# Two more combined pairs in the feed-forward's first part of a hybrid encoder step, and two weight sums of every combined pair made by adding transfers

## The chip, the cores and the metric

The kernel runs on 1 core of a Trainium2 chip. The metric is the device time of one execution in microseconds. Engine names: PE is TensorE, DVE is VectorE, ACT is ScalarE, POOL is GpSimd, SP is SyncE, which here only issues transfers.

## The reference, cut to what matters

Two layers. Each projects 640 rows (512 prompt rows, 8 x 16 sample rows) of 1024 features, runs two attention branches, mixes them with gates and closes with the feed-forward part that is at issue here:

```python
def finish_layer(x, a, b, ga, gb, w_a, w_b, w_o, g1, b1, w_up, w_down, g2, b2):
    mix = (ga * (a @ w_a) + gb * (b @ w_b)) @ w_o
    x = layer_norm(ALPHA * x + mix, g1, b1)
    h = jnp.square(jax.nn.relu(x @ w_up)) @ w_down      # 1024 -> 4096 -> 1024
    return layer_norm(ALPHA * x + h, g2, b2)
```

All arrays are float32, D_MODEL is 1024, D_FF 4096, DEPTH 2.

## The kernel before, in words

**Products in halves.** Every float32 operand is split into a high part (rounded by a copy to fp32r, ACT) and a low part (the rest, a subtraction, DVE). A product is three matmuls that add up in PSUM: high x high, low x high, high x low. Weights come as chunks of 128 x 1024 (512 KB), two chunks (a pair n) at a time, into four raw slots (`load`, L489); SP loads a slot again when the low part of the chunk in it has been made (`w_ready`).

**Plain tiles.** `feature_tile` (L549 to L551) multiplies one chunk (128 output features) with all 640 rows, as two halves of 320 rows, 8 blocks of 128 inputs each.

**Combined pairs.** `combined_pair` on PE (L575 to L577) takes two chunks together as a 2 x 2 block matrix (two output tiles, two halves of the inputs, two halves of the rows) and makes it with seven block products in place of eight, by sums of blocks: four x sums t1 to t4 (made once and kept, `x_sums`, `x_sum_low`, `t_high`) and four weight sums per pair. The seven products, in order, go to five PSUM banks X1 to X5: X1 (part 0), X4 (part 1, the sum s_one, with t1), X2 (part 2, t2), X1 (part 3), X2 (part 4, t3), X3 (part 5), X5 (part 6, t4). ACT copies a bank into another between them (`up_seed`, L1600: seed 0 is X1 to X2 after the first product, seed 1 X2 to X3 after the third, seed 2 X2 to X5 after the fifth), and the later product adds onto the copy. The third product waits for seed 0, the fifth for seed 1, the seventh for seed 2. DVE makes the sums (`weight_sums`: L2400 s_one = a21 + a22, L2403, L2407, L2411), ACT the high parts (`part_highs`, L1573), DVE the low parts (`part_low`, L2420). s_one has one buffer. Each pair's weights are made during the pair before; the first pair's of a group before the group starts.

**The order.** Each engine's program is written out by hand and runs in order, with counted semaphores between them. Per layer: first head and v tiles, 4 combined pairs of gates, 8 heads of attention, 4 combined pairs of the branch product (BRANCH), window attention, second branch, mix and layer norm, then the feed-forward in 4 parts. A part makes 8 tiles of up features (4 pairs), squares of their relu, and multiplies them with 8 chunks of w_down (`row_group`, L642 to L644). In part 0 the four pairs are plain; in parts 1 to 3 they are combined. In part 0 ACT does relu (L1842) and the high part of the square (L1845), DVE the square (L2658) and its low part (L2661), and in between the x sums of that layer (L2359 to L2375, high parts L1539, low parts L2385) for part 1. Part 0's first pair is run by `first_tiles`, between the last transposes of the layer norm (L933), from weights kept aside; the second starts right behind it. GpSimd has no program of its own.

The lines of ACT's program for part 0:

```python
for u in range(FF_PAIRS):
    for s in range(2):
        act.wait_ge(chunk_done[s], nth(l, AT_FF) + u + 1)
        fn(halves(tmp1[:]), pair(s), ACT.Relu).then_inc(relu_done[s], 1)
        high(s, nth(l, AT_FF, 1) + u)
        fn(act_a[0][:, 2 * u + s, :], tmp2[:], ACT.Copy).then_inc(h_hi_ready, 1)
    for t in ((), (1,), (2, 3), (4,))[u]:
        t_high(l, 1, t)
```

## Time and profile before

| | us |
|---|---|
| median of 3 runs | 2186.23 (2185.57 to 2189.0) |
| the profiled execution | 2187.18 |
| its span | 2185.4 |
| PE busy | 2175.2 |
| DVE busy | 1408.0 |
| ACT busy | 1135.6 |
| POOL busy | 0.2 |

The span is the time from the first to the last record of the profiled execution. Busy is the time in which an engine had an instruction in work. Matmuls are pipelined, so a record (309 ns for 320 columns) overlaps the next; the distance from one start to the next is what one costs. A wait is put down to the engine that released it.

### The profile page before, as it was taken

Reading aid. Unit: us, or ns where it says so; the run is one execution under the profiler, and the core shown is the slowest. Engines: PE = TensorE matmul, PEld = TensorE weight load, DVE = VectorE, ACT = ScalarE, POOL = GpSimd, SP = SyncE. Lnnn points to the kernel's source line nnn. Section 1 sums busy time; section 2 is a strip of 40 time slices with the busy share of each in tenths; the row PEclk is TensorE's granted clock in tenths of the full one; section 3 lists DMA queues with packets and bytes.
Section 4 is the critical chain, followed back from the end, with each engine's and each line's share of the span. In section 5 each row is a group of like instructions: output and inputs, shape, how many; then the busy total and the mean of one; then the engine's idle time right before and its main releaser. Section 6 shows DMA issues by size and latency. Waiting matters only on the chain.

```text
span 2185.4 us, 38374 instructions
## 1 busy us (share of the span) xinstructions
PE 2175.2 (100%) x15290; PEld 1981.7 (91%) x15290; DVE 1408.0 (64%) x2324; ACT 1135.6 (52%) x2401; POOL 0.2 (0%) x4
## 2 busy tenths in 40 slices
PE   9999999999999999999999999999999999999998
PEld 8988889999989898989889888899999898989897
DVE  6757777776466573736667577786764665736466
ACT  4457776686323262626234677666853232626261
POOL 0000000000000000000000000000000000000000
PEclk9999999999999999999999999999999999999999
DMA  5366552431431222222233765525214312222231
GB/s 186 102 243 253 200 214 101 151 111 50 147 119 39 87 78 83 86 74 88 106 108 103 275 233 191 206 86 172 74 51 148 116 54 79 85 73 88 68 111 73
DMA packets 68160, 268.18 MB, mean 123 GB/s; under 512 B 10984, under 2 KB 12648, under 8 KB 61296
## 3 DMA queue, kind: packets, MB, share of 16 engines
q1 hardware_dynamic: 43136, 152.75, 20.5%
q10 hardware_dynamic: 24848, 112.99, 14.5%
q8 instruction: 122, 2.00, 0.4%
q14 instruction: 54, 0.44, 0.1%
HBM read 236.35 MB, written 25.95 MB: 120 GB/s over the span
## 4 chain that ended last, share of the span: by engine, by line
PE 99%; DVE 0%; DMA 0%; DVEq 0%; issue 0%; ACT 0%; ACTq 0%
PE PS L549 11%; PE PS L551 11%; PE PS L550 11%; PE PS L642 10%; PE PS L644 10%; PE PS L643 10%; PE PS L575 8%; PE PS L577 8%; PE PS L576 8%; PE PS L768 2%; PE PS L793 2%; PE PS L732 1%; PE PS L683 1%; PE PS L898 1%; PE PS L782 1%; PE PS L714 1%
## 5 line engine op out<-in xcount | busy, mean ns | idle before, releaser
L549 PE MATMUL PS<-xt_hi,w_hi 128*128 128x320 f32 x1312 | 420.7, 321 | 0.0
L551 PE MATMUL PS<-xt_hi,w_lo 128*128 128x320 f32 x1312 | 405.3, 309 | 0.0
L550 PE MATMUL PS<-xt_lo,w_hi 128*128 128x320 f32 x1312 | 405.1, 309 | 0.0
L1128 ACT ACTIVATE w_hi<-w_raw 128x1024 fp32r<-128x1024 f32 x194 | 203.6, 1058 | 361.8 <-PE PS L644 286.0
L1914 DVE TENSOR_TENSOR w_lo<-w_raw,w_hi 128x1024 fp32r<-128x1024 f32 x194 | 235.4, 1222 | 235.9 <-ACT w_hi L1128 232.3
L642 PE MATMUL PS<-w_hi,act_a_hi 128*128 128x512 f32 x800 | 312.2, 390 | 0.0
L644 PE MATMUL PS<-w_hi,act_a_lo 128*128 128x512 f32 x800 | 311.4, 389 | 0.0
L643 PE MATMUL PS<-w_lo,act_a_hi 128*128 128x512 f32 x800 | 311.4, 389 | 0.0
L549 PEld LDWEIGHTS PS<-xt_hi,w_hi 128*128 128x128 f32 x1312 | 246.6, 188 | 10.6 <-issue 8.0
L550 PEld LDWEIGHTS PS<-xt_lo,w_hi 128*128 128x128 f32 x1312 | 246.9, 188 | 0.1
L551 PEld LDWEIGHTS PS<-xt_hi,w_lo 128*128 128x128 f32 x1312 | 246.3, 188 | 0.0
L644 PEld LDWEIGHTS PS<-w_hi,act_a_lo 128*128 128x128 f32 x800 | 150.2, 188 | 31.5
L642 PEld LDWEIGHTS PS<-w_hi,act_a_hi 128*128 128x128 f32 x800 | 150.2, 188 | 30.9 <-issue 0.5
L643 PEld LDWEIGHTS PS<-w_lo,act_a_hi 128*128 128x128 f32 x800 | 150.2, 188 | 30.5
L1155 ACT ACTIVATE rope_s<-PS 32x320 f32<-32x320 f32 x352 | 150.6, 428 | 49.5 <-DVE z_all L1905 22.8
L2420 DVE TENSOR_TENSOR part_lo<-w_raw,part_hi 128x512 fp32r<-128x512 f32 x130 | 88.7, 689 | 57.1 <-ACT part_hi L1573 54.2
L1573 ACT ACTIVATE w_hi<-w_raw 128x512 fp32r<-128x512 f32 x110 | 66.3, 624 | 59.3 <-PE PS L644 48.5
L1573 ACT ACTIVATE part_hi<-w_raw 128x512 fp32r<-128x512 f32 x130 | 80.1, 623 | 27.9 <-DVE w_raw L2407 26.8
L2257 DVE SCALAR_TENSOR_TENSOR rows<-rows,PS 128x512 f32<-128x512 f32 x100 | 67.2, 685 | 34.0 <-PE PS L644 34.0
L575 PE MATMUL PS<-t_hi,part_hi 128*128 128x320 f32 x288 | 89.0, 309 | 0.0
L576 PE MATMUL PS<-t_lo,part_hi 128*128 128x320 f32 x288 | 89.0, 309 | 0.0
L577 PE MATMUL PS<-t_hi,part_lo 128*128 128x320 f32 x288 | 89.0, 309 | 0.0
(282 smaller groups left out, 4574.0 us busy)
## 6 DMA issues: line engine op xcount, KB each, us to landing
w_raw<-in_weights SPq DMA_DIRECT2D x274, 512.0 KB, 3.5
kc<-in_k_cache ACTq DMA_DIRECT2D x32, 1024.0 KB, 7.7
vc<-in_v_cache ACTq DMA_DIRECT2D x16, 2048.0 KB, 8.8
gates_kept<-a_t ACTq DMA_DIRECT2D x8, 640.0 KB, 7.0
k_out<-k_t ACTq DMA_DIRECT2D x16, 320.0 KB, 2.4
v_out<-rows ACTq DMA_DIRECT2D x2, 2560.0 KB, 16.9
mix_a<-a_t ACTq DMA_DIRECT2D x2, 2560.0 KB, 11.7
rope_c<-gates_kept ACTq DMA_DIRECT2D x10, 320.0 KB, 3.2
```

Of the source, the lines that this page charges most:

```text
L549: mm(out, wh, hi[:, k, c], start=(k == 0), stop=False)
L550: mm(out, wh, lo[:, k, c], start=False, stop=False)
L551: last = mm(out, wl, hi[:, k, c], start=False, stop=(k == KT - 1))
L575: mm(up_bank(x), wh, moving[0][:, k], start=first and k == 0, stop=False, skip_group_check=True)
L576: mm(up_bank(x), wh, moving[1][:, k], start=False, stop=False, skip_group_check=True)
L577: last = mm(up_bank(x), wl, moving[0][:, k], start=False, stop=(k == KH - 1), skip_group_check=True)
L642: mm(out, xh, wh, start=(k == 0), stop=False)
L643: mm(out, xh, wl, start=False, stop=False)
L644: last = mm(out, xl, wh, start=False, stop=(k == KT - 1))
L1128: fn(w_hi[slot][:], raw[:, j, :], ACT.Copy).then_inc(w_hi_made[s], 1)
L1155: last = fn(rope_s[dst:dst + 32, half * HALF:(half + 1) * HALF], PS[src:src + 32, bank_of(0, half), 0:HALF], ACT.Copy, scale=scale)
L1914: v.tensor_tensor(w_lo[slot][:], raw[:, raw_of(s, n)[0], :], w_hi[slot][:].bitcast(F32), ALU.subtract)\
```

## The change

Part 0 of the feed-forward runs its pairs 0 and 1 plain and its pairs 2 and 3 combined, in both layers, so that there are 44 combined pairs in place of 40. PSUM bank three (X2) holds other results until then, so one extra matmul with the start flag opens it ahead of the first combined pair of part 0. The x sums are made within the first two pairs. ACT now makes both squares of a plain tile's relu (the high part and the full square), and DVE only the low part.

Of the four weight sums of every combined pair, s_one and s_three (the sum in place of a21) are no longer made by DVE but by transfers of GpSimd's queue, which add in flight: `weights[2n, :, 0:512]` is added onto the raw slot of the second chunk, and s_one is loaded with a21, and after that has landed a22 is added. As a transfer can only add, the signs of two sums, of t3 and of two seeds are turned, and the takes (`up_add`) subtract where they added. Three semaphores of the attention heads become one. Cut to its core:

```diff
-BRANCH = FF_PARTS
-PAIR_ORDER = (0, BRANCH, 1, 2, 3)
-PAIR_GROUPS = len(PAIR_ORDER)
+PLAIN_PAIRS = 2
+GATES, BRANCH = FF_PARTS, FF_PARTS + 1
+
+
+def first_pair(part):
+    return 0 if part else PLAIN_PAIRS
+
+
+PAIR_ORDER = [(part, u) for part in (GATES, BRANCH, 0, 1, 2, 3) for u in range(first_pair(part), FF_PAIRS)]
+LAYER_PAIRS = len(PAIR_ORDER)
...
+        @block.gpsimd
+        def _(pool):
+            def pair_sums(l, part, u):
+
+                q, n = pair_at(l, part, u)
+                j, loads = raw_of(1, n)
+                pool.wait_ge(raw_loaded[j], 16 * loads)
+                pool.dma_start(raw[:, j, 0:BANK], weights[2 * n, :, 0:BANK], accum_op=ALU.add)\
+                    .then_inc(s_three_added, 16)
+                if q:
+                    pool.wait_ge(s_summed, 2 * q - 1)
+                    pool.wait_ge(part_ready, 5 * q - 3)
+                if (part, u) == (GATES, 0):
+                    if l == 0:
+                        pool.wait_ge(masks_ready, 2)
+                        pool.wait_ge(lam_link, 6)
+                    else:
+                        pool.wait_ge(input_rows, l * ROW_STEPS)
+                elif (part, u) == (BRANCH, 0):
+                    pool.wait_ge(unit_pv, 3 * HEADS * (l + 1))
+                    pool.wait_ge(dec_ms_ready, HEADS * (l + 1))
+                elif (part, u) == (0, PLAIN_PAIRS):
+                    pool.wait_ge(ln_rows, ROW_STEPS * (l + 1))
+                pool.dma_start(s_one[:], weights[2 * n + 1, :, 0:BANK]).then_inc(s_one_loaded, 16)
+                pool.wait_ge(s_one_loaded, 32 * q + 16)
+                pool.dma_start(s_one[:], weights[2 * n + 1, :, BANK:D], accum_op=ALU.add).then_inc(s_one_loaded, 16)
+
+            for l in range(DEPTH):
+                for part, u in PAIR_ORDER:
+                    pair_sums(l, part, u)
...
+                if renew is not None:
+                    pe.wait_ge(x_lo_ready, renew)
+                    mm(up_bank(X2), part_hi[0][:, 0:P], b11[0][:, 0], start=True, stop=True)
...
-                        if part > 0:
-                            if (part, u) == (1, 0):
-                                pe.wait_ge(t_lo_ready, sums_before(l + 1, 0))
-                                for s in range(2):
-                                    pe.wait_ge(relu_done[s], (l + 1) * FF_PAIRS)
+                    if part == 0:
+                        for u in range(1, PLAIN_PAIRS):
+                            for s in range(2):
+                                pe.wait_ge(relu_done[s], l * PLAIN_PAIRS + u)
+                                feature_tile(s, nth(l, AT_FF) + u, xt_hi, xt_lo, s)
+                    for u in range(first_pair(part), FF_PAIRS):
+                        if part == 0 and u == PLAIN_PAIRS:
+                            first_waits = {0: lambda: pe.wait_ge(relu_done[0], (l + 1) * PLAIN_PAIRS),
+                                           1: lambda: pe.wait_ge(relu_done[1], (l + 1) * PLAIN_PAIRS),
+                                           KH: lambda: None}
+                            combined_pair(*pair_at(l, part, u), sums_before(l, 2), first_waits=first_waits,
+                                          renew=tiles_before(l, 1) + ROW_STEPS)
+                        else:
                             combined_pair(*pair_at(l, part, u))
-                        elif u > 0:
-                            for s in range(2):
-                                pe.wait_ge(relu_done[s], l * FF_PAIRS + u)
...
+            def up_tile(l, u, s):
+
+                t = l * 2 * PLAIN_PAIRS + 2 * u + s
+                tile = tmp2 if s else tmp1
+                act.wait_ge(chunk_done[s], nth(l, AT_FF) + u + 1)
+                if u:
+                    act.wait_ge(h_ready, l * 32 + 2 * u + s - 1)
+                fn(halves(tile[:]), pair(s), ACT.Relu).then_inc(relu_done[s], 1)
+                if u + 1 < PLAIN_PAIRS:
+                    high(s, nth(l, AT_FF, 1) + u)
+                act.wait_ge(relu_done[s], l * PLAIN_PAIRS + u + 1)
+                fn(act_a[0][:, 2 * u + s, :], tile[:], ACT.Square).then_inc(h_hi_ready, 1)
+                act.wait_ge(h_hi_ready, t + 1)
+                fn(tile[:], tile[:], ACT.Square).then_inc(sq_done, 1)
...
-                for u in range(FF_PAIRS):
-                    for s in range(2):
-                        t = l * 8 + 2 * u + s
-                        act.wait_ge(chunk_done[s], nth(l, AT_FF) + u + 1)
-                        act.wait_ge(sq_done, t)
-                        fn(halves(tmp1[:]), pair(s), ACT.Relu).then_inc(relu_done[s], 1)
-                        high(s, nth(l, AT_FF, 1) + u)
-                        wait_apart(act, sq_done, t + 1)
-                        fn(act_a[0][:, 2 * u + s, :], tmp2[:], ACT.Copy).then_inc(h_hi_ready, 1)
-                    for t in ((), (1,), (2, 3), (4,))[u]:
-                        t_high(l, 1, t)
+                up_tile(l, 0, 0)
+                t_high(l, 1, 1)
+                up_tile(l, 0, 1)
+                part_highs(l, 0, PLAIN_PAIRS, (0,))
+                t_high(l, 1, 2)
+                t_high(l, 1, 3)
+                up_tile(l, 1, 0)
+                part_highs(l, 0, PLAIN_PAIRS, (1, 2, 3))
+                up_tile(l, 1, 1)
+                part_highs(l, 0, PLAIN_PAIRS, (4,))
+                t_high(l, 1, 4)
+                part_highs(l, 0, PLAIN_PAIRS, (6, 5))
...
-                if which == 1:
-                    for s in range(2):
-                        j, loads = raw_of(s, n)
-                        dve.wait_ge(raw_loaded[j], 16 * loads)
-                    if q:
-                        dve.wait_ge(s_summed, 4 * q - 1)
-                        dve.wait_ge(part_ready, 5 * q - 3)
-                    v.tensor_tensor(s_one[:], a21, a22, ALU.add).then_inc(s_summed, 1)
-                elif which == 3:
-                    dve.wait_ge(s_summed, 4 * q + 1)
-                    v.tensor_tensor(a21, a11, a21, ALU.subtract).then_inc(s_summed, 1)
-                elif which == 2:
-                    dve.wait_ge(s_summed, 4 * q + 2)
+                first = raw[:, raw_of(0, n)[0], :]
+                a11, a12 = first[:, 0:BANK], first[:, BANK:D]
+                if which == 2:
+                    dve.wait_ge(s_one_loaded, 32 * (q + 1))
                     dve.wait_ge(part_ready, 5 * q + 1)
-                    v.tensor_tensor(a11, s_one[:], a11, ALU.subtract).then_inc(s_summed, 1)
+                    v.tensor_tensor(a11, s_one[:], a11, ALU.add).then_inc(s_summed, 1)
                 elif which == 4:
-                    dve.wait_ge(s_summed, 4 * q + 3)
+                    dve.wait_ge(s_summed, 2 * q + 1)
                     dve.wait_ge(part_ready, 5 * q + 4)
-                    v.tensor_tensor(a12, a12, a11, ALU.subtract).then_inc(s_summed, 1)
+                    v.tensor_tensor(a12, a12, a11, ALU.add).then_inc(s_summed, 1)
...
-                weight_sums(l, part, 0, 1)
-                weight_sums(l, part, 0, 3)
-                part_low(l, part, 0, 0)
-                weight_sums(l, part, 0, 2)
+                u = first_pair(part)
+                part_low(l, part, u, 0)
+                weight_sums(l, part, u, 2)
                 for o in (1, 2, 3):
-                    part_low(l, part, 0, o)
-                weight_sums(l, part, 0, 4)
-                part_low(l, part, 0, 4)
+                    part_low(l, part, u, o)
+                weight_sums(l, part, u, 4)
+                part_low(l, part, u, 4)
...
-                for u in range(FF_PAIRS):
-                    for s in range(2):
-                        t = 2 * u + s
-                        dve.wait_ge(relu_done[s], l * FF_PAIRS + u + 1)
-                        dve.wait_ge(h_ready, l * 32 + t)
-                        v.tensor_tensor(tmp2[:], tmp1[:], tmp1[:], ALU.mult).then_inc(sq_done, 1)
-                        low(s, nth(l, AT_FF, 1) + u)
-                        dve.wait_ge(h_hi_ready, l * 8 + t + 1)
-                        v.tensor_tensor(act_a[1][:, t, :], tmp2[:], act_a[0][:, t, :].bitcast(F32),
-                                        ALU.subtract).then_inc(h_ready, 1)
-                    x_sums(l, 1, u)
+                def up_tile_low(u, s):
+
+                    t = 2 * u + s
+                    dve.wait_ge(sq_done, l * 2 * PLAIN_PAIRS + t + 1)
+                    v.tensor_tensor(act_a[1][:, t, :], (tmp2 if s else tmp1)[:], act_a[0][:, t, :].bitcast(F32),
+                                    ALU.subtract).then_inc(h_ready, 1)
+
+                x_sums(l, 1, 1)
+                low(0, nth(l, AT_FF, 1))
+                up_tile_low(0, 0)
+                x_sums(l, 1, 2)
+                low(1, nth(l, AT_FF, 1))
+                up_tile_low(0, 1)
+                part_low(l, 0, PLAIN_PAIRS, 0)
+                weight_sums(l, 0, PLAIN_PAIRS, 2)
+                x_sum_low(l, 1, 1)
+                part_low(l, 0, PLAIN_PAIRS, 1)
+                x_sums(l, 1, 3)
+                x_sum_low(l, 1, 2)
+                part_low(l, 0, PLAIN_PAIRS, 2)
+                part_low(l, 0, PLAIN_PAIRS, 3)
+                weight_sums(l, 0, PLAIN_PAIRS, 4)
+                x_sum_low(l, 1, 3)
+                part_low(l, 0, PLAIN_PAIRS, 4)
+                up_tile_low(1, 0)
+                part_low(l, 0, PLAIN_PAIRS, 5)
                 x_sum_low(l, 1, 4)
+                part_low(l, 0, PLAIN_PAIRS, 6)
+                up_tile_low(1, 1)
```

## Rows read from the trace of the kernel before

**Rows 1.** The page, busy time of each engine, and granted clock in 40 slices.

```profile
PE 2175.2 (100%) x15290; PEld 1981.7 (91%) x15290; DVE 1408.0 (64%) x2324; ACT 1135.6 (52%) x2401; POOL 0.2 (0%) x4
...
PEclk9999999999999999999999999999999999999999
```

**Rows 2.** Waits of PE: who waited for whom, us in total, times, longest.

```profile
PE PS L982 <- DVE mask_cols L2548: 1.5, 1, 1.5
PE PS L974 <- DVE xt_lo L2561: 0.8, 1, 0.8
```

**Rows 3.** Stretches: a plain pair, a combined pair; length, busy us (instructions), PEclk, DMA.

```profile
682.67:696.75 14.08, 14.08 (x99) 14.08 (x98) 5.89 (x7) 4.78 (x6) 0.00 (x0) 1.00 0.33 113
804.10:816.42 12.32, 12.32 (x86) 12.32 (x85) 9.53 (x15) 9.84 (x20) 0.00 (x0) 1.00 0.27 86
```

**Rows 4.** Timeline of PE: start us, duration us; pair 2 of part 0, of part 1.

```profile
696.74 0.31 PE L549 MATMUL PS<-xt_hi,w_hi 128*128 128x320 f32 x1
...
803.97 0.31 PE L575 MATMUL PS<-xt_hi,part_hi 128*128 128x320 f32 x1
```

**Rows 5.** Timeline of ACT, part 0 of the feed-forward; in brackets the idle time before.

```profile
679.34 0.70 ACT L1842 ACTIVATE rope_c<-PS 128x640 f32<-128x640 f32 x1 [4.23 <-PE PS L551]
...
689.90 0.70 ACT L1842 ACTIVATE rope_c<-PS 128x640 f32<-128x640 f32 x1 [4.62 <-PE PS L551]
...
696.94 0.70 ACT L1842 ACTIVATE rope_c<-PS 128x640 f32<-128x640 f32 x1 [4.62 <-PE PS L551]
...
717.63 2.68 ACT L1539 ACTIVATE t_hi<-t 128x1280 fp32r<-128x1280 f32 x2 [4.18 <-DVE t L2368]
720.21 0.69 ACT L1842 ACTIVATE rope_c<-PS 128x640 f32<-128x640 f32 x1
...
1783.92 0.70 ACT L1842 ACTIVATE rope_c<-PS 128x640 f32<-128x640 f32 x1 [4.62 <-PE PS L551]
```

**Rows 6.** Timeline of DVE, the same part.

```profile
675.14 0.69 DVE L2245 TENSOR_TENSOR xt_lo<-PS,xt_hi 128x512 fp32r<-128x512 f32 x1 [0.35 <-ACT xt_hi L1173]
...
681.03 1.23 DVE L1914 TENSOR_TENSOR w_lo<-w_raw,w_hi 128x1024 fp32r<-128x1024 f32 x1
...
702.02 1.49 DVE L2361 TENSOR_TENSOR t<-b,xt_hi 128x1280 f32<-128x1280 f32 x1
...
717.52 1.48 DVE L2369 TENSOR_TENSOR t<-b,b 128x1280 f32<-128x1280 f32 x1
```

**Rows 7.** Timeline of ACT in combined pairs, branch group first, then part 1.

```profile
399.89 0.63 ACT L1573 ACTIVATE part_hi<-s_one 128x512 fp32r<-128x512 f32 x1
...
792.06 0.74 ACT L1692 ACTIVATE act_a_hi<-rope_c 128x640 fp32r<-128x640 f32 x1
792.83 0.74 ACT L1697 ACTIVATE rope_c<-rope_c 128x640 f32<-128x640 f32 x1
...
794.32 0.43 ACT L1600 ACTIVATE PS<-PS 128x320 f32<-128x320 f32 x1
...
809.08 0.62 ACT L1573 ACTIVATE part_hi<-s_one 128x512 fp32r<-128x512 f32 x1
```

**Rows 8.** Timeline of DVE in combined pairs, the last readers of s_one.

```profile
391.22 0.68 DVE L2420 TENSOR_TENSOR part_lo<-s_one,part_hi 128x512 fp32r<-128x512 f32 x1
...
798.71 0.69 DVE L2420 TENSOR_TENSOR part_lo<-s_one,part_hi 128x512 fp32r<-128x512 f32 x1
```

**Rows 9.** Groups of DVE: busy us, mean ns, idle before; one of four sums.

```profile
L2400 DVE TENSOR_TENSOR s_one<-w_raw 128x512 f32<-128x512 f32 x40 | 27.3, 684 | 0.0
```

**Rows 10.** Transfers by line: count, KB each, median us from issue to landing.

```profile
w_raw<-in_weights SPq DMA_DIRECT2D x274, 512.0 KB, 3.5
...
w_raw<-in_weights SPq DMA_DIRECT2D x2, 256.0 KB, 5.3
s_v<-in_swa_vc ACTq DMA_DIRECT2D x2, 256.0 KB, 6.7
x_all<-rows SPq DMA_DIRECT2D x2, 256.0 KB, 2.1
```

More of the change, by code:

```diff
@@ L559, in a_blocks, with combined_pair @@
                 return [(aq_hi[:, i], aq_lo[:, i]) for i in range(3)]
-            def combined_pair(q, n, sums=None, blocks=None, t_hi=t_hi, t_lo=t_lo, first_waits=None):
+            def combined_pair(q, n, sums=None, blocks=None, t_hi=t_hi, t_lo=t_lo, first_waits=None,
+                              renew=None):
                 def x_sum_ready(t):
@@ L1851, in _ @@
                         part_highs(l, part, 0, range(7))
-                        for u in range(FF_PAIRS):
-                            combined_pair(l, part, u)
+                    for u in range(first_pair(part), FF_PAIRS):
+                        combined_pair(l, part, u)
                     if part < FF_PARTS - 1:
@@ L2132, in branch_pair @@
                 last = u == FF_PAIRS - 1
-                if not last:
-                    weight_sums(l, BRANCH, u + 1, 1)
-                    weight_sums(l, BRANCH, u + 1, 3)
-                else:
+                if last:
                     part_low(l, BRANCH, u, 4)
@@ L2375, in x_sums @@
                     v.tensor_tensor(full[4], full[4], lo[1][0], ALU.add).then_inc(t_ready, 1)
-                    if not which:
-                        low(1, nth(l, AT_V, 3))
-                    x_sum_low(l, which, 2)
-                    x_sum_low(l, which, 3)
             def x_sum_low(l, which, t):
@@ L2487, in combined_pair @@
                 last = u == FF_PAIRS - 1
+                first = first_pair(part)
                 down = nth(l, AT_FF, 4) + part * 8
-                if not last:
-                    weight_sums(l, part, u + 1, 1)
-                    weight_sums(l, part, u + 1, 3)
-                if u > 0:
+                if u > first:
                     up_low(l, part, u - 1, 0)
```

187 lines of the change are left out of this document (96 added, 91 removed).

## The prediction

> **What bounds the kernel now.** I read the page's busy line first: TensorE is busy for 2175.2 of the 2185.4 us of the span, and its granted clock is in the top tenth in all 40 slices [rows 1]. Then the waits of TensorE by name: two in the whole run, 1.5 and 0.8 us, both in the first microseconds [rows 2]. So nothing else in the kernel reaches the path: a matmul removed is time removed, work of VectorE or ScalarE removed is nothing, and every new wait of TensorE counts in full. Third, two stretches [rows 3]: a plain pair of up tiles (two tiles, 2 halves x 8 blocks x 3 terms each = 96 matmuls of 320 columns) fills 14.08 us and a combined pair (7 products x 4 blocks x 3 terms = 84) fills 12.32 us. Both give 0.1467 us a matmul; the 309 ns of a record is latency, not its price. Last, the timelines of ScalarE and VectorE in the first part of the feed-forward and in a combined pair, since the change rewrites what they do there. Times below are layer 0's; layer 1 repeats them 1087 us later (its fourth relu at 1783.9 against 696.94 [rows 5]).
>
> **1. Fewer products.** Pairs 2 and 3 of part 0 become combined in both layers: 4 pairs x (14.08 - 12.32) = 7.04 us less. The opening of bank three adds one matmul per layer, 2 x 0.147 = 0.29 us. Net -6.75 us.
>
> **2. A new wait at the first combined pair of part 0.** Today pair 2 begins at 696.74 [rows 4], and needs only its banks and weights. In the changed kernel its third product adds onto bank three, and waits for the first seed (ScalarE's copy from the first product's bank). TensorE asks for it after the opening matmul and two products: 696.74 + 0.15 + 24 x 0.1467 = 700.41. ScalarE works in order, and before this seed its program has: relu of tile 3 (it can start when pair 1's last matmul is done, 696.94), two squares of it, high part 4, the high part of x sum 4, high parts 6 and 5. Durations: relu 0.70, the 128x1280 high part 1.27 (half of its row), squares 0.74 each as the combined pairs have them, parts 0.62, seed 0.43 [rows 5, 7]. Sum 0.70 + 2 x 0.74 + 3 x 0.62 + 1.27 + 0.43 = 5.74 us. Consecutive instructions overlap by about 0.1 us (717.63 + 2.68 is 720.31, the next starts at 720.21 [rows 5]), but one that waits for its own predecessor starts 0.03 after its end (792.06 to 792.83 [rows 7]); five overlaps and two such waits give 5.3 us, and the seed ends at 702.27. TensorE loses 702.27 - 700.41 = 1.86, with the semaphore 1.9 us per layer, 3.8 us in both. Bounds: 1.4 if all steps overlap, 2.6 if none does and a part high waits for VectorE. In the steady state the seed has only 0.4 us to spare (that of the second pair of part 1 ends at 794.75 [rows 7]; its pair starts 12.32 before 803.97 [rows 4], so its product is due at 791.65 + 24 x 0.1467 = 795.17), so 3.7 us of extra work ahead of it cannot vanish. After the wait the delay is kept and not repeated: pair 3 runs 1.9 us later relative to both engines.
>
> **3. VectorE in the first part.** It is free from 675.83 [rows 6]. In the new order: three steps of x sum 1 of 1.5 us (to 680.4), low part of the next tile when its high part is there (681.03 to 682.26), tile 0's low (to 683.3), then three steps of x sum 2 and 3, of 1.49 each [rows 6] (to 687.6), and only then the low part of pair 1's second tile, 1.23 us, to 688.8. TensorE wants it at 696.74 - 48 x 0.1467 = 689.70. 0.9 us of margin remains. Going on in the same way the x sums' and parts' low halves end at 697.8 and 698.5 for the third product, wanted at 700.41, at 701.2 and 701.8 for the fifth, wanted at about 705.8, and at 705.2 for the last, wanted at 709.4. None is late: 0. The thin place is later: ScalarE's third high part of pair 3 waits for a sum that VectorE gives at 707.2, and the third seed of pair 2, behind it, ends at 709.1 against 709.4. The bounds are 0 and 1 us per layer; below nothing it cannot go, as TensorE waits nowhere here now [rows 2].
>
> **4. Weight sums by transfers.** VectorE loses 2 x 0.684 us per pair (40 pairs) [rows 9], which is cover, not path: 0. Instead the GpSimd queue issues for each of 44 pairs an adding transfer into the raw slot, a 256 KB load of the one-buffered sum s_one, and, when that has landed, an adding transfer of 256 KB onto it. Queued on GpSimd behind the raw slot's load and behind these waits are only the next pair's transfers; on the other side wait ScalarE's high part 1 (and behind it the second seed and all later seeds, in order) and VectorE's second sum. The window for load plus addition runs from the last read of s_one, the low part of the pair before, to ScalarE's high part. There are three such windows in each of the ten groups of today. The shortest kind in the feed-forward, at the fourth pair of a part, is 799.40 to 809.08 [rows 7, 8], 9.7 us (the second and third pairs' are some 2 us longer); the shortest of all, in the branch group, is 391.90 to 399.89, 8.0 us. ScalarE may still be later without TensorE noticing: in the fourth pair's case the second seed must end at 803.97 [rows 4] + 48 x 0.1467 = 811.0, high part and seed take 0.95, so the high part may start at 810.05: 10.65 us allowed. In the branch it is about 10.0. No such transfer is in the trace. Nearest rows: 512 KB from the same weights land 3.5 us after issue, 256 KB transfers 2.1 (a store), 5.3 (at the crowded start) and 6.7 us (beside the window cache's other load) [rows 10]. So load and addition cost from 2 x 2.1 = 4.2 to 2 x 6.7 = 13.4 us. I take the weight row, the same source in the same stage: 2 x 3.5 = 7.0 us, inside 10. The first addition needs the raw slot loaded; that load is issued when the slot's last low part is done, lands 3.5 us later and is ahead of the window's start by then or within 1 us of it. First pairs of a group have tens of us. So: 0.
> The Trainium skill, DMA: Bandwidth & Descriptors, section "Anatomy of one DMA — SWDGE (gpsimd) path", gives a fixed 2.0 us plus bytes over 436e3, by which a 256 KB transfer would be an estimated 2.6 us and the chain 5.2; it prices no addition, and no row here shows this queue.
> The Trainium skill, SBUF — State Buffer, section "Who interferes with whom", speaks against the change: GpSimd cannot write descriptors while VectorE runs a two-port instruction. It also says that tensor_tensor, which is what VectorE runs in these pairs, has no such mode; no run here has shown either yet.
>
> **5. The rest.** Sign flips of seeds, sums and takes and the merged unit semaphores change no count and no order: 0. Squares of the plain tiles go from VectorE to ScalarE, which is idle 4 us ahead of each relu there (its waits for TensorE before the relus at 679.34 and 689.90 are 4.2 and 4.6 us [rows 5]); inside that idle time, except as counted in part 2.
>
> **The sum.** -6.75 + 3.8 = -2.95 us. The profiled execution took 2187.18 us (span 2185.4 and 1.8 around it), which gives 2184.2; the median of the runs shown, 2186.23, is 0.95 lower, so the forecast is 2183.3 us, 0.13% below. What this kernel's measurement can tell from no change is 0.2%, 4.4 us: faster is below 2181.9, slower above 2190.6.
>
> **Rivals.**
> A: the seed is in time. Then only part 1 counts: 2186.23 - 6.75 = 2179.5. For it: TensorE waits for nobody anywhere today. Against it: the order of ScalarE's program and the durations in part 2, all from rows. It would take five instructions gone from between 697 and 702.
> B, on the slower side: load plus addition of s_one takes longer than its window. From about 10 us per chain on it decides; every further microsecond is paid at the fourth pair of each part (8 times) and twice in the branch. At 11.5 us (3.5 for the load, 8 for an addition that reads and writes) that is 8 x 0.85 + 2 x 1.5 = 9.8 us, 2193.1; at the upper bound of 13.4 the third pairs join and it is about 35 us, 2218. For it: the chain of two with a wait between, one buffer, no row of this queue. Against: the weight row, 7.0, and VectorE's two sums fewer, which bring the last read of s_one forward.
> C: the thin margins of part 3 break as well (0.9 us at pair 1's second tile, 0.3 at the third seed), up to 1.5 us per layer: 2184 to 2187.
>
> **How the numbers follow.** Forecast 0.55 (its own range 2181.3 to 2185.0, of which 0.08 falls below 2181.9), A 0.20, C 0.12, B 0.13. Faster 0.08 + 0.20 = 0.28, within 0.2% 0.47 + 0.12 = 0.59, slower 0.13. The range takes in A, the forecast and C and leaves out most of B: 2179.0 to 2189.0.
>
> **What would show it.** TensorE's waits should have exactly one new kind, at the third product of part 0's first combined pair, released by ScalarE's seed, about 1.9 us, twice. The first combined pair of part 0 should span 14.2 to 14.5 us with the wait, the second 12.3. The adding transfers should land within 3 to 4 us each, and ScalarE's high part of s_one should wait for none of them. Wrong would be: no such wait (A), waits of TensorE behind seeds in third and fourth pairs of all groups (B), or a wait at pair 1's second tile (C).

## The result, and the profile after

The changed kernel took 2208.03 us (median of four runs, 2202.67 to 2211.65) against 2186.15 for the kernel before on the same chip: slower, ratio 1.0096 with a 95% interval of 1.0083 to 1.0109. The forecast was 2183.3, its range ended at 2189.0, and slower had a chance of 0.13.

The profiled execution took 2208.8 us. Its page, to be laid beside [rows 1]: span, busy times, granted clock in 40 slices, GpSimd's own queue (packets, MB, share of the transfer engines), and the chain that ended last.

```profile
span 2206.8 us, 38420 instructions
...
PE 2176.1 (99%) x15244; PEld 1980.3 (90%) x15244; DVE 1365.2 (62%) x2264; ACT 1159.3 (53%) x2461; POOL 100.9 (5%) x136
...
PEclk9999999999999999999999999999999999999999
...
q0 software_dynamic: 16192, 34.61, 8.3%
...
PE 74%; issue 14%; DMA 6%; DVE 4%; POOL 1%; ACT 1%; DVEq 0%; ACTq 0%; POOLq 0%
```

TensorE has 46 matmuls less, which is what was counted (4 x 12 - 2), and yet the span grew by 21.4 us. The chain of waits, which was TensorE alone before, now has transfers in it. The waits of TensorE, against [rows 2]:

```profile
PE PS L620 <- ACT PS L1656: 16.1, 8, 4.1
PE PS L620 <- DVE w_lo L2476: 3.5, 2, 1.8
PE PS L1030 <- DVE mask_cols L2599: 1.6, 1, 1.6
```

The second line is the forecast's new wait, twice, at part 0's first combined pair. It is put down to VectorE, but the matmul starts at 714.28 and ScalarE's seed ends at 714.17; it is the seed. With the wait this pair spans 14.46 us and the next one 12.32, as forecast (14.2 to 14.5, and 12.3). The third line, at the very start, is in [rows 2] too. The first line was forecast at nothing: a product waits for a seed of ScalarE. One of its places, in the branch group, in TensorE's timeline (start us, us; idle before it in brackets):

```profile
408.45 0.31 PE L622 MATMUL PS<-aq_hi,part_lo 128*128 128x320 f32 x1
412.60 0.38 PE L620 MATMUL PS<-ta_hi,w_hi 128*128 128x320 f32 x1 [3.85 <-ACT PS L1656]
...
413.43 0.47 PE L622 MATMUL PS<-ta_hi,w_lo 128*128 128x320 f32 x1
413.69 0.47 PE L620 MATMUL PS<-ta_hi,w_hi 128*128 128x320 f32 x1
```

In ScalarE's timeline the seed stands behind the high part of the next pair's s_one, and that one waited 5.8 us for the transfer:

```profile
411.50 0.63 ACT L1627 ACTIVATE part_hi<-s_one 128x512 fp32r<-128x512 f32 x1 [5.79 <-DMA s_one<-in_weights]
...
412.04 0.42 ACT L1656 ACTIVATE PS<-PS 128x320 f32<-128x320 f32 x1
```

VectorE's last read of s_one ahead of it, and then GpSimd's three issues of this pair, each in its engine's timeline:

```profile
395.81 0.69 DVE L2476 TENSOR_TENSOR part_lo<-s_one,part_hi 128x512 fp32r<-128x512 f32 x1
```

```profile
399.83 0.86 POOL L552 DMA_DIRECT2D w_raw<-in_weights  x1 [11.20 <-DMA w_raw<-in_weights]
400.37 0.89 POOL L568 DMA_DIRECT2D s_one<-in_weights  x1
406.47 0.86 POOL L570 DMA_DIRECT2D s_one<-in_weights  x1 [5.21 <-DMA s_one<-in_weights]
```

s_one is free at 396.50. Its load goes out at 400.37, 3.9 us later, because the addition for s_three (S3, line 552) stands ahead of it in GpSimd's queue and waits for the raw slot to land; this delay is called the hold below. The addition onto s_one can go out 6.1 us after the load's issue, and has landed 5.0 us after its own: from 396.50 to 411.50 are 15.0 us, where the forecast had 10 allowed and 7.0 needed. The same happens at 98.46 and 1182.14 in the gates group (15.5 and 15.7 us) and at 1495.84 in the branch (15.3). In each of the four the hold is only a part (2.4, 3.9, 2.4 and 4.4 us, in order of time); load and addition take 13.1, 11.1, 13.3 and 10.9. At the first of them the addition goes out within 0.2 us of two other transfers, and lands 8.0 us later:

```profile
103.38 0.33 SPq L501 DMA_DIRECT2D w_raw<-in_weights  x1
103.51 0.40 ACTq L1696 DMA_DIRECT2D gates_kept<-a_t  x1
103.56 0.85 POOL L570 DMA_DIRECT2D s_one<-in_weights  x1 [4.20 <-DMA s_one<-in_weights]
```

The stretches of and behind such idles (length; PE busy us and matmuls; granted clock; share of the transfer engines; GB/s):

```profile
108.70:112.60 3.90, 0.00 (x0) 1.00 0.34 67
113.08:116.50 3.42, 3.42 (x14) 0.51 0.00 0
408.60:412.60 4.00, 0.15 (x2) 1.00 0.79 121
413.43:416.80 3.37, 3.37 (x14) 0.50 0.46 143
```

Behind each of these two idles of 4 us TensorE gets half its clock (1.2 of 2.4 GHz) for 3.4 us: 14 matmuls, where 3.4 us hold 23 at full clock.

The account of the profiled run, from the distances between the starts of 320-column matmuls: idles over 0.3 us sum up to 21.3 us (3.9 of them the two forecast ones; four of 2.9 to 4.3 us in the gates and branch groups are 15.3; four of 0.5 to 0.6, three of them in the feed-forward), distances of a slowed clock to 24.4 us against 18.5 before, so 5.9 more (5.2 of it right behind three of the four long idles). -6.75 + 21.3 + 5.9 = 20.5 of the 21.4 us by which the span grew; 0.9 is not placed.

### The profile page after: what moved, and what is told of

It reads as the page before. It is cut to its first block, busy times and chain, and to the rows that moved or that the text cites. A ratio compares the mean times of both kernels' runs of the same rounds, so it can differ in the third digit from the quotient of the medians.

```text
span 2206.8 us, 38420 instructions
## 1 busy us (share of the span) xinstructions
PE 2176.1 (99%) x15244; PEld 1980.3 (90%) x15244; DVE 1365.2 (62%) x2264; ACT 1159.3 (53%) x2461; POOL 100.9 (5%) x136
## 4 chain that ended last, share of the span: by engine, by line
PE 74%; issue 14%; DMA 6%; DVE 4%; POOL 1%; ACT 1%; DVEq 0%; ACTq 0%; POOLq 0%
PE PS L593 9%; PE PS L594 8%; PE PS L595 8%; PE PS L691 7%; PE PS L690 7%; PE PS L692 7%; DMA s_one<-in_weights 6%; PE PS L620 5%; PE PS L621 5%; PE PS L622 5%; PE PS L816 2%; PE PS L841 2%; PE PS L780 1%; PE PS L731 1%; PE PS L946 1%
## 5 line engine op out<-in xcount | busy, mean ns | idle before, releaser
L593 PE MATMUL PS<-xt_hi,w_hi 128*128 128x320 f32 x1184 | 381.2, 322 | 0.1
L595 PE MATMUL PS<-xt_hi,w_lo 128*128 128x320 f32 x1184 | 365.8, 309 | 0.0
L594 PE MATMUL PS<-xt_lo,w_hi 128*128 128x320 f32 x1184 | 365.5, 309 | 0.0
L593 PEld LDWEIGHTS PS<-xt_hi,w_hi 128*128 128x128 f32 x1184 | 222.6, 188 | 10.9 <-issue 7.8
L594 PEld LDWEIGHTS PS<-xt_lo,w_hi 128*128 128x128 f32 x1184 | 222.9, 188 | 0.1
L595 PEld LDWEIGHTS PS<-xt_hi,w_lo 128*128 128x128 f32 x1184 | 222.3, 188 | 0.0
L552 POOL DMA_DIRECT2D w_raw<-in_weights x44 | 38.0, 864 | 1774.0 <-DMA w_raw<-in_weights 1739.3
L620 PE MATMUL PS<-t_hi,part_hi 128*128 128x320 f32 x328 | 101.5, 309 | 3.5 <-DVE w_lo L2476 3.5
L622 PE MATMUL PS<-t_hi,part_lo 128*128 128x320 f32 x328 | 101.4, 309 | 0.0
L621 PE MATMUL PS<-t_lo,part_hi 128*128 128x320 f32 x328 | 101.3, 309 | 0.0
```

The costliest lines, as they stand in the source:

```text
L593: mm(out, wh, hi[:, k, c], start=(k == 0), stop=False)
L594: mm(out, wh, lo[:, k, c], start=False, stop=False)
L595: last = mm(out, wl, hi[:, k, c], start=False, stop=(k == KT - 1))
L620: mm(up_bank(x), wh, moving[0][:, k], start=first and k == 0, stop=False, skip_group_check=True)
L621: mm(up_bank(x), wh, moving[1][:, k], start=False, stop=False, skip_group_check=True)
L622: last = mm(up_bank(x), wl, moving[0][:, k], start=False, stop=(k == KH - 1), skip_group_check=True)
```

## The experiments

Fifteen kernels. The ratio is to the kernel before, timed along with each (median 2186.4 to 2187.4 us), with its 95% interval. An idle is given as the distance between two starts of TensorE less the 0.147 us of a matmul. By the forecast's own terms 2187 - 6.75 is 2180.3 with no wait at all.

**Both sums by VectorE** (`e1`): the GpSimd block goes, the two new combined pairs stay.

```
+ v.tensor_tensor(s_one[:], raw[:, j, 0:BANK], raw[:, j, BANK:D], ALU.add).then_inc(s_one_loaded, 1)
+ v.tensor_tensor(a21, a11, a21, ALU.add).then_inc(s_three_added, 1)
```

> Both weight sums of every combined pair are made by VectorE again, no transfer adds; the two new combined pairs stay. Theory (the pairs are worth what was counted, the transfers are the whole loss): products -6.75, the wait for seed 0 of part 0 +3.85 (two idles of 1.93 us), no idle over 1 us in the gates and branch groups, granted clock .999; 2186.2 - 6.75 + 3.85 = 2183.3 us. Rival (the new pairs or the bank opened anew cost more than the wait, e.g. VectorE's thin margins or the clock): 2187 us or more.

2191.71 us, ratio 1.0023 (1.0014 to 1.0032). The rival: no idle in the gates and branch groups, but part 0 has a second one, in both layers. Timelines of TensorE, ScalarE and VectorE:

```profile
705.64 0.31 PE L590 MATMUL PS<-xt_hi,part_lo 128*128 128x320 f32 x1
708.47 0.38 PE L588 MATMUL PS<-t_hi,w_hi 128*128 128x320 f32 x1 [2.52 <-issue]
```

```profile
707.42 0.63 ACT L1595 ACTIVATE part_hi<-s_one 128x512 fp32r<-128x512 f32 x1 [4.44 <-DVE s_one L2446]
707.95 0.42 ACT L1624 ACTIVATE PS<-PS 128x320 f32<-128x320 f32 x1
```

```profile
705.96 0.82 DVE L2708 TENSOR_TENSOR act_a_lo<-rope_s,act_a_hi 128x640 fp32r<-128x640 f32 x1
706.70 0.69 DVE L2446 TENSOR_TENSOR s_one<-w_raw 128x512 f32<-128x512 f32 x1
```

VectorE is busy without a gap up to there and makes s_one late, ScalarE's high part waits for it, and the second seed behind that is late by 2.7 us. So 2 x (1.92 + 2.68) = 9.2 us, and 1.6 of a slower clock behind the idle in layer 0: -6.75 + 10.8 = +4.1, measured +4.7. The pairs alone make the kernel slower; the transfers give VectorE its time back just there.

**Early seed** (`e2`): as `e1`, with seed 0 ahead of four of the seven instructions of step 2 (high 4, the high of x sum 4, highs 6 and 5); the relu and its two squares stay ahead of it.

```
  up_tile(l, 1, 1)
+ up_seed(l, 0, PLAIN_PAIRS, 0)
  part_highs(l, 0, PLAIN_PAIRS, (4,))
```

> As the kernel with both sums by VectorE, and seed 0 of part 0's first combined pair issued right after the high part of channel tile (1,1), ahead of six ScalarE instructions. Theory (the 1.93 us idle at the third product is that queue and nothing else): both idles gone, 2186.2 - 6.75 = 2179.5 us. Rival (what is moved behind the seed, high 4 and highs 6 and 5, is late in turn): the idle moves to the next products, 2182 to 2184 us.

2193.74 us, ratio 1.0032 (1.0020 to 1.0044): the rival by kind, but 10 us above it. The expectation counts six instructions; the edit has four. The idle at the third product is gone and the one at the fifth is now 4.7 us (1.92 + 2.68 = 4.60): the time is kept whole, moved into one piece, and both layers now get the half clock behind it (busy us and instructions of TensorE, its weight loads, VectorE, ScalarE and GpSimd, then as above):

```profile
707.50:710.70 3.20, 3.20 (x13) 3.20 (x13) 2.68 (x4) 1.73 (x4) 0.00 (x0) 0.50 0.07 28
1797.50:1803.00 5.50, 5.50 (x22) 5.50 (x22) 3.77 (x6) 2.37 (x5) 0.00 (x0) 0.50 0.03 13
```

**Load first** (`e3`): GpSimd issues the load of s_one ahead of the S3 addition; nothing else is changed.

```
+ pool.dma_start(s_one[:], weights[2 * n + 1, :, 0:BANK]).then_inc(s_one_loaded, 16)
  pool.wait_ge(raw_loaded[j], 16 * loads)
  pool.dma_start(raw[:, j, 0:BANK], weights[2 * n, :, 0:BANK], accum_op=ALU.add)
- pool.dma_start(s_one[:], weights[2 * n + 1, :, 0:BANK]).then_inc(s_one_loaded, 16)
```

> As the changed kernel, but GpSimd issues the load of s_one ahead of the S3 addition, which waits for the raw slot to land. Theory (of the chain, the 2 to 4.4 us that the load is held behind that wait decides, and without it the chain fits the window at most pairs): the 4 us idles and the falls of the clock gone, idles of at most 1 us, 2183 to 2190 us. Rival (the two transfers in a row are too long by themselves, 11 us and more beside the other loads of the gates and branch groups): idles of 2 to 4 us stay at those pairs, 2195 to 2206 us.

2186.43 us, ratio 1.0000 (0.9990 to 1.0009), as the theory said. Of the changed kernel's loss of 22 us all is gone by moving one issue. That move takes two things from ahead of the load: the wait for the raw slot, and S3's own bytes. The same pair as above, VectorE's last read and then GpSimd:

```profile
390.01 0.69 DVE L2476 TENSOR_TENSOR part_lo<-s_one,part_hi 128x512 fp32r<-128x512 f32 x1
```

```profile
391.27 0.57 POOL L564 DMA_DIRECT2D s_one<-in_weights  x1 [8.81 <-DVE part_lo L2476]
393.94 0.87 POOL L567 DMA_DIRECT2D w_raw<-in_weights  x1 [2.10 <-DMA w_raw<-in_weights]
394.57 1.13 POOL L570 DMA_DIRECT2D s_one<-in_weights  x1
```

The load goes out 0.57 us after the read (3.87 in the changed kernel) and lets the addition go 3.3 us later (6.1); the high part comes 11.2 us after the read and costs TensorE 0.3 us. Over all pairs the median from the load's issue to the addition's is 3.33 us here and 4.69 in the changed kernel, and the load is held 0.57 us at every pair whose window is short, against a median of 1.9 and up to 4.36 in the changed kernel.

**The addition left out** (`e6`): the changed order, s_one by its load alone (its second summand is missing).

> As the changed kernel, with the addition to s_one left out (the second summand is missing in that weight sum, so the output is another); its load of 256 KB and the S3 addition stay, in the order of the changed kernel. Theory (the loss is the length of the chain of two transfers): with one transfer in the chain the window holds it at every pair, 2183 to 2185 us. Rival (the hold behind the raw slot together with contention for the DMA engines is enough by itself, or the added traffic slows the raw loads): idles of 1 us or more stay in the gates and branch groups, 2188 us or more.

2185.95 us, ratio 0.9996 (0.9986 to 1.0005), 1 us above the theory's range. Beside part 0's idles there are two of 0.4 and 0.6 us in the branch. One transfer fits the window even with the hold: it is the hold and the chain of two transfers together that break it.

**One sum by transfer, the other by VectorE.** `e4`: s_one by transfers, S3 by VectorE. `e5`: the other way round.

> s_one by load and addition on GpSimd's queue, S3 by VectorE: no instruction that waits for the raw slot stands ahead of the load. Theory (hold and chain together make the idles): the load goes out when the last reader of s_one ends, the chain starts 2 to 4 us earlier at the late pairs, idles of at most 1 us, 2183 to 2190 us. Rival (the chain alone is too long): 2195 us or more.

> S3 by the adding transfer into the raw slot, s_one by VectorE: no chain of two transfers for one sum. Theory (S3's addition lands long before its reader, and costs nothing): idles as with both sums by VectorE, 2183.3 us. Rival (the addition, which can begin only when the raw slot has landed, is itself late, or an adding transfer takes the DMA engines from the raw loads): 2187 us or more.

`e4` 2185.66 us, ratio 0.9995 (0.9986 to 1.0005), and `e5` 2187.48, 1.0004 (0.9995 to 1.0014). Neither has an idle over 0.3 us outside part 0. In `e4` nothing of S3 is in GpSimd's queue, and at the four places named above load and addition take 7.2 to 8.2 us. The idle at part 0's fifth product is 0.62 us in `e4` and 1.83 in `e5`, against 2.68 with both sums by VectorE and none in `e3`. So `e5`'s own expectation of 2183.3 missed: it needs the time of VectorE that s_one's transfer gives.

**S3 last** (`e11`): load, addition, then the S3 addition.

> The changed kernel with the S3 addition as the last of the three transfers of a pair. Load-first gave chains of 6.3 to 8.3 us and a load that landed 2.7 us after its issue (4.7 us behind the S3 addition). Theory (what stands ahead of the load in GpSimd's queue is the loss): chains as with the load first or shorter, the same time, 2184 to 2187 us. Rival (the S3 addition, now after the wait for the first load and the issue of the second, comes too late for high 4): new waits of the fourth high on S3, 1 us or more at some pairs, 2188 us or more.

2189.36 us, ratio 1.0014 (1.0005 to 1.0023), between theory and rival. Figures in this expectation and in that of the next experiment were misread from another issue: from the load's issue "2.7 us" is 3.3, and the chains of "6.3 to 8.3 us" are 7.2 to 10.6. No high part waited for S3. Two idles of 2.4 and 1.7 us came in the branch, where ScalarE stood at another transfer: `rope_c` from `gates_kept`, 3.5 us.

```profile
1492.20 0.74 ACT L1742 ACTIVATE rope_c<-rope_c 128x640 f32<-128x640 f32 x1 [3.52 <-DMA rope_c<-gates_kept]
...
1494.20 0.42 ACT L1656 ACTIVATE PS<-PS 128x320 f32<-128x320 f32 x1
```

In these groups a transfer moved beside the gates' loads delays them as well; whether it does so by its bytes alone was not isolated.

**Small S3** (`e16`): the changed order, S3 adds 4 of its 512 columns (the rest of it is not added).

```
- pool.dma_start(raw[:, j, 0:BANK], weights[2 * n, :, 0:BANK], accum_op=ALU.add)
+ pool.dma_start(raw[:, j, 0:4], weights[2 * n, :, 0:4], accum_op=ALU.add)
```

> The changed kernel in its own order (S3 addition, load, addition), but the S3 addition adds only 4 of its 512 columns: the rest of S3 is not added, so the output is another. GpSimd waits for the raw slot as before, the bytes of that transfer are gone. Theory H (the load is late because GpSimd's queue stands at the wait for the raw slot): the load still goes out 2 to 4 us late at the latest pairs, idles of 2 to 4 us stay, 2200 us or more. Theory Q (the bytes ahead of it in the DMA queue make it late: it landed 4.7 us after its issue behind the S3 addition and 2.7 us ahead of it): it lands after 2.7 to 3 us, idles shrink by 2 us each, 2188 to 2196 us.

2199.97 us, ratio 1.0062 (1.0044 to 1.0079). Both share: 8 us of the 22 go with the bytes (the load takes 3.60 us in the median instead of 4.69), and some 14 stay with the wait. The split is rough, since the runs of either kernel spread over 8 to 9 us. Idles of 2.1, 4.0 and 4.9 us remain in the gates and branch groups, one of 1.0 in the feed-forward, and the same pair still looks like this:

```profile
393.37 0.86 POOL L552 DMA_DIRECT2D w_raw<-in_weights  x1 [11.22 <-DMA w_raw<-in_weights]
393.90 0.89 POOL L568 DMA_DIRECT2D s_one<-in_weights  x1
397.54 0.86 POOL L570 DMA_DIRECT2D s_one<-in_weights  x1 [2.74 <-DMA s_one<-in_weights]
```

The load is held 3.7 us there, and the addition needed 8.6, although no S3 bytes are ahead. Its neighbours are again two other transfers, issued up to 0.4 us ahead of it:

```profile
397.21 0.33 SPq L501 DMA_DIRECT2D w_raw<-in_weights  x1
397.25 0.35 ACTq L1738 DMA_DIRECT2D rope_c<-gates_kept  x1
```

In `e4` the same addition goes out 2.6 us ahead of the transfer of `rope_c` and lands in 4.2 us. By these traces the hold costs twice: it starts the chain late, and it pushes the addition among transfers that it would have been ahead of. No run takes these neighbours away alone, so that they are the reason for the 8 us is not shown.

**Second seed first** (`e7`): the changed kernel, ScalarE makes the second seed ahead of the next pair's high 1.

```
  up_fifth(l, part, u)
  if not last:
+     up_seed(l, part, u, 1)
      part_highs(l, part, u + 1, (1,))
```

> The changed kernel, and in every combined pair ScalarE makes the second seed, which the fifth product waits for, ahead of the high part of the next pair's s_one instead of behind it; GpSimd's order stays as changed. In the changed kernel the 4.0 us idle at 408.45 ended with that seed at 412.04, and the high ahead of it in ScalarE's queue came at 411.50, when s_one had landed. Theory (the late sum stops TensorE only through ScalarE's queue, some 7 us before a product needs it): the idles at the fifth products go; what is left is the third seed, behind the highs 2 and 3 in the same queue, 1 to 3 us at the two or three latest pairs, and 3.85 us at part 0; 2186 to 2195 us. Rival (the sum itself is needed there): no difference, 2205 us or more.

2199.0 us, ratio 1.0054 (1.0037 to 1.0071). 9 us back. The idles at the fifth products are gone, those of the feed-forward too; at the seventh there are now 3.6, 2.8, 2.1, 1.0, 0.7 and 0.6 us, because the third seed stands behind highs 1 to 3. The theory had the place right and the size too small, by 4 us.

**Second and third seed first** (`e10`; the kernel before it is `e7`):

> As the kernel before it in this call, with the third seed too ahead of the next pair's highs 1, 2 and 3. Theory (with no seed behind a wait for s_one the window grows by the three products and the next pair's first, four times 1.76 us, and holds the changed kernel's chain of up to 13.6 us): no idle over 1 us in the gates and branch groups, 2183 to 2186 us. Rival (the highs, made some 5 us later, let the lows, the raw slots and the loads slip, so the wait turns up at the lows or at the slots): idles of 1 to 3 us in all groups, 2190 us or more.

2230.34 us, ratio 1.0201 (1.0185 to 1.0216): the rival, and far worse. The highs, made later, run into ScalarE's squares and push seed 0 behind them, 26 waits of TensorE:

```profile
PE PS L620 <- ACT PS L1654: 32.1, 26, 1.8
```

**VectorE's sums with the second seed first** (`e9`), to see what bounds part 0:

> Both sums by VectorE, and the second seed ahead of the next pair's high 1 in ScalarE's queue. With both sums by VectorE part 0 had two idles, 1.92 us at the third product and 2.68 us at the fifth, where the second seed stood behind a high that waited for VectorE's s_one. Theory (VectorE's queue, filled without a gap from 697 to 711 us, is the bound there, the seeds only show it): the 2.68 us idle moves to the seventh product, 2.5 us there, 2189 to 2192 us. Rival (the order of ScalarE's queue alone): the idle goes, 2183 to 2185 us.

2190.56 us, ratio 1.0017 (1.0008 to 1.0027). As the theory said, the 2.68 us idle moved to the seventh product, and is 2.26 there.

**Load first, second seed first, early seed 0** (`e8`), and **the same with the third seed of that one pair ahead of high 2** (`e14`):

> Load of s_one ahead of the S3 addition; second seed ahead of the next pair's high 1; seed 0 of part 0's first combined pair right after the high of channel tile (1,1). Theory (both idles of part 0, 1.93 us in either layer, and the four of 0.5 to 0.8 us go, nothing takes their place while VectorE has two sums fewer per pair): 2187.0 - 6.75 = 2180 us. Rival (as with both sums by VectorE, the idle moves to the next seed, because VectorE or the following highs are late): 2183 to 2186 us.

> The kernel with the load first, the second seed first and the early seed 0, and at part 0's first combined pair the third seed too ahead of the next pair's high 2 (which waited 3.46 us for VectorE's sum, with an idle of 1.88 us at the seventh product). Theory (the lows of the next pair were ready at 706.3 to 707.9, before its first product could start even without the idle, so only the seed's place holds TensorE): the idles go in both layers, 3.76 us, profile about 2180, median 2182 us. Rival (VectorE's burst is the bound, the idle moves once more): 2185 to 2187 us.

`e8` 2185.89 us, ratio 0.9997 (0.9988 to 1.0006); `e14` 2185.79, 0.9998 (0.9988 to 1.0007). Both are the rival's case. In `e8` the two idles of 1.9 us are at the seventh product, since high 2 ahead of the seed waits for VectorE's sum:

```profile
705.73 0.63 ACT L1628 ACTIVATE part_hi<-w_raw 128x512 fp32r<-128x512 f32 x1 [3.46 <-DVE w_raw L2468]
...
707.10 0.43 ACT L1657 ACTIVATE PS<-PS 128x320 f32<-128x320 f32 x1
```

In `e14` they are 1.56 us, at the third product of the second combined pair, behind ScalarE's squares:

```profile
709.62 0.74 ACT L1765 ACTIVATE act_a_hi<-rope_c 128x640 fp32r<-128x640 f32 x1
710.39 0.74 ACT L1770 ACTIVATE rope_c<-rope_c 128x640 f32<-128x640 f32 x1
...
711.88 0.43 ACT L1657 ACTIVATE PS<-PS 128x320 f32<-128x320 f32 x1
```

**Transfers in the feed-forward only**, once with everything else as in `e14` (`e15`) and once as in the changed kernel (`e17`):

```
- for part, u in PAIR_ORDER:
+ for part, u in PAIR_ORDER[8:]:
      pair_sums(l, part, u)
```

> As the kernel before it in this call, with the transfers in the feed-forward's pairs only; in the gates and branch groups VectorE makes both sums. Theory (the transfers cost only where the other loads of these groups lengthen the chain, and in the feed-forward they buy VectorE's time in part 0): as the kernel before or up to 2 us below, 2179 to 2182 us. Rival (the transfers cost a small amount wherever they are, by contention that no idle shows): no difference to the kernel before.

> The changed kernel in its own order (S3 addition first, seeds where they were), with the transfers in the feed-forward's pairs only; in the gates and branch groups VectorE makes both sums. Theory (the changed kernel's loss lies in these two groups, where the other loads lengthen a chain that the wait for the raw slot has already put off): 2187.1 - 6.75 + 3.85 + idles of 0.3 to 0.6 us at some fourth pairs of the feed-forward, some 2 us in all: 2186 us, clock .999. Rival (the order of GpSimd's queue costs as much in the feed-forward, its idles only overlap with others there): 2192 us or more.

`e15` 2182.45 us, ratio 0.9980 (0.9971 to 0.9989), the fastest of all and faster than the kernel before: its slowest run (2184.38) lies below that kernel's fastest (2185.56). `e17` 2184.68, ratio 0.9988 (0.9978 to 0.9997), 1 us below its theory and far from its rival. `e15` is 3.3 us below `e14`; the trace of `e14` shows only one idle of 0.6 us in the branch to explain it, but it is of the fastest of that kernel's ten runs, so most of the difference has no trace. The changed kernel's own order (`e17`) costs the feed-forward three idles of 0.3 to 0.8 us; its 22 us lie in the gates and branch groups. TensorE's waits in `e15`:

```profile
PE PS L637 <- ACT PS L1674: 2.8, 2, 1.4
PE PS L1047 <- DVE mask_cols L2651: 1.6, 1, 1.6
PE PS L1039 <- DVE xt_lo L2664: 0.9, 1, 0.9
```

## Why the prediction was wrong, step by step

**What bounds it** was right: every wait of TensorE counted in full, and the distances between its starts account for the time.

**Step 1**, fewer products: right, 46 matmuls, -6.75 us.

**Step 2**, the seed's wait, 1.86 to 1.9 us per layer: right in place, cause and size. From the first of the seven instructions ahead of the seed in ScalarE's timeline (708.88) to the seed's end (714.17) are 5.3 us, as summed. Rival A had the seed in time. `e2`, `e8` and `e14` put it in time by order, and it does not help: the idle moves, in `e8` and `e14` 3.1 to 3.8 of the 3.85 us stay, and in `e2` all of it. VectorE is busy for 14.2 of the 15 us from 700 to 715 in the changed kernel and ScalarE for 11.1; in `e8` ScalarE's high 2 waits 3.5 us for VectorE.

**Step 3**, VectorE's margins in part 0: nothing was late, as forecast, but only because the transfers had taken its two sums; `e1` shows that with them there the second idle is 2.68 us per layer. Step 4 put them down as cover, worth 0.

**Step 4**, the weight sums by transfers, costed at 0, is the one that failed, in two terms that only together are too much.

The first is the hold. The step said of the raw slot's load that it "lands 3.5 us later and is ahead of the window's start by then or within 1 us of it". In the kernel before that was so: at the branch pair shown above it went out at 388.60 and landed 4.0 us later, 0.75 us after s_one was free (391.90). In the changed kernel it went out only 2.0 us ahead of that moment and landed 5.0 us after its issue (394.52 to 399.55, against 396.50). The load of s_one then went out 2.0 to 4.4 us late at the third pairs of the gates and branch groups (and the fourth of layer 0's gates). In parts 1 to 3 of the feed-forward it was 1.9 to 3.6 us late at the second and third pairs, where the windows had nearly all the room for it. The forecast counted what waits behind GpSimd's issues and put almost nothing on what the load itself stands behind.

The second is the size of the chain, 2 x 3.5 = 7.0 us. Alone in GpSimd's queue it is about that: 7.4 us in the median of `e4`. Behind S3's bytes the load takes 4.7 us and not 3.3, and the addition, 3.9 to 4.1 at the best, takes 5.3 in the median where it was waited for, and up to 8.2 in the gates group. At the four long idles the chain was 10.9 to 13.3 us, so it was off by 3.9 to 6.3 us there, more than the hold. It is so long mostly because of the order, though: the same four chains are 7.3 to 10.6 us in `e3`, and 7.2 to 8.2 in `e4`. The order of the three issues is the cause that `e3`, `e4`, `e6` and `e16` show; which transfers slow a late chain, and by how much, is open.

The bounds, 4.2 to 13.4 us, held for load plus addition (up to 13.3 at 1182.14), but not for the window as a whole, which had the hold in front. The allowance of 10 us in the branch was 1 us too small: at 15.0 the idle was 4.0, so 11.0 were allowed.

**Rival B** is what happened, by mechanism (a chain longer than its window, seen at ScalarE's second seed), but with its weight in the gates and branch groups and not at the fourth pairs of the feed-forward, and with the hold in front and a price that it did not have: the clock behind long idles, 5.2 us here. Its chance, 0.13, was too small for a step with no row of its queue in the trace; its upper case, 13.4 us and 2218, was closer than the forecast.

**Rival C** did not happen: TensorE has no idle at pair 1's second tile or at the third seed.

Of the two rules quoted: the Trainium skill, DMA: Bandwidth & Descriptors, section "Anatomy of one DMA — SWDGE (gpsimd) path", gave an estimated 2.6 us for 256 KB. In `e4`, with nothing of GpSimd's ahead, the load landed after 3.0 us in the median and released the next issue after 3.3; so the estimate is too low for this use by 0.4 to 0.7 us, and by more for an addition, which it did not price (4.1 us in the median of `e4`). The Trainium skill, SBUF — State Buffer, section "Who interferes with whom", warned of descriptors held back by VectorE; the issues of GpSimd took 0.56 to 1.2 us each in all these kernels, also beside VectorE's tensor_tensor, which the page excepts. No run here shows such a stop.

**What made a better kernel** was to leave the sums with VectorE in the groups where transfers are dense and VectorE has time, and to give them to transfers where VectorE is full: `e15`, 0.20% below the kernel before. Against `e17` it has 2.2 us less of idle in the feed-forward, which is the order of the issues and the seeds there. Its profiled run took 2181.53 us: -6.75 for the products and +3.1 for the idles left give 2183.5 from the 2187.18 of before. Of the other 2 us 1.6 lie at the very start: from 5.9 to 9.9 us the kernel before gets 15 matmuls done, `e15` 26, though both show a full granted clock there. Of the seventeen profiled executions seven have 24 to 27 matmuls in this stretch and ten 13 to 16, and kernels with and without the transfers are among both, so this part is not put down to `e15`. The runs of the kernel before lie near 2185.6 or near 2187.4 us, which would fit, but there is one trace of it; the cause stays open.

```profile
5.90:9.90 4.00, 3.94 (x15) 1.00 0.99 361
```

```profile
5.90:9.90 4.00, 3.82 (x26) 1.00 0.99 367
```

(The first line is the kernel before, the second `e15`; columns as in the stretches above: length, TensorE's busy us and matmuls, granted clock, share of the transfer engines, GB/s.)

## What to carry to other kernels

When work moves to a queue that runs in order, list for each issue what stands ahead of it and when that is released, not only what stands behind: one wait for an unrelated buffer ahead of a chain cost some 14 us here and the bytes behind that wait 8 more, and moving one issue gave all of it back. An engine far from the path by its average (VectorE, busy 65% of the span in `e1`) can be the bound in one stretch of 15 us; where moving a wait only moves the idle, look for the engine that is full there. And a transfer that has no row in the trace needs a trial or a wide range, above all in stages where the transfer engines are already in use.

## What the runs showed of the hardware that was not expected

A transfer of 256 KB of GpSimd's queue released the next issue 3.3 us after its own, 4.7 with another 256 KB adding transfer ahead of it in the queue, 3.6 with a tiny one ahead. An adding transfer of 256 KB onto on-chip memory landed 3.9 us after its issue at best and 4.1 in the median of `e4`, where the plain load took 2.8 and 3.0. Issued within 0.4 us of two transfers of other queues it took 8.0 and 8.6 us.

Behind idles of TensorE the granted clock fell to 0.5 and stayed there for 3.4 to 6 us, at a price of 1.5 to 2.8 us each. It did so behind all idles of 3.6 to 4.9 us. In the range below, it fell behind one of 2.7 us (`e1`, layer 0, where another of 1.9 had ended 3.6 us before) and not behind the same two in layer 1; behind single ones of 2.1 to 2.4 us (`e7`, `e11`, `e16`); behind five of the twelve idles of 2.0 us in `e10`; and not behind those of 2.8 and 2.9 us (`e7`, and 1193.55 in the changed kernel). So the length of the idle alone does not decide in that range, and what else does stays open.
